# Attention's probabilities times V on narrower TensorE tiles: 12 products a head group instead of 6

## What is computed

```python
SEQ, CHUNK = 256, 64
ATTN_HEADS, ATTN_KV_HEADS, ATTN_HEAD_DIM = 16, 2, 64
# sliding window of 128 keys, in chunks of 64 queries
scores = jnp.einsum('bnqhgd,bnkhd->bnhgqk', qc, kb).astype(jnp.float32) * (ATTN_HEAD_DIM ** -0.5)
...
probs = jax.nn.softmax(jnp.concatenate([scores, sink], axis=-1), axis=-1)[..., :-1]
out = jnp.einsum('bnhgqk,bnkhd->bnqhgd', probs.astype(vb.dtype), vb)
return out.reshape(B, S, ATTN_WIDTH)
```

## Time and profile before

| | |
|---|---|
| median of three runs | 1077.94 us (1077.86 to 1078.0) |
| the profiled execution, own time | 1078.6 us |
| its span, first to last instruction | 1076.9 us |
| TensorE busy | 1072.4 us, 6575 matmuls and 6575 weight loads |
| VectorE, ScalarE, GpSimd busy | 909.0, 635.2, 79.8 us |
| granted TensorE clock, mean | 1.000 of full speed |
| all of `times_v`, as busy time of its two lines | 2.6 us (L2026) and 2.4 us (L2030) |

### The profile page before, as it was taken

The page is one execution under the profiler, slowest core; times in us unless marked ns, Lnnn a source line. Parts: engine busy times, 40 slices in busy tenths (PEclk is TensorE's granted clock), DMA queues, the critical chain, the costliest instruction groups (busy, mean ns, idle before and its releaser), DMA issues.

```text
span 1076.9 us, 18252 instructions
## 1 busy us (share of the span) xinstructions
PE 1072.4 (100%) x6575; PEld 928.2 (86%) x6575; DVE 909.0 (84%) x1376; ACT 635.2 (59%) x930; POOL 79.8 (7%) x114
## 2 busy tenths in 40 slices
PE   9999999999999999999999999999999999999998
PEld 9888888888888888888888888888888888888887
DVE  6878988989655678888888888888877889999997
ACT  7677676756545655555555555545555566656663
POOL 4500000000000000000000000000000000000000
PEclk9999999999999999999999999999999999999999
DMA  8656587877889888798888888789887789798884
GB/s 270 189 165 188 177 231 223 220 226 217 234 268 246 267 246 238 239 252 236 249 230 245 247 247 248 221 255 253 272 236 236 222 280 325 260 303 313 260 296 157
DMA packets 192336, 260.77 MB, mean 242 GB/s; under 512 B 9605, under 2 KB 143894, under 8 KB 192022
## 3 DMA queue, kind: packets, MB, share of 16 engines
q1 hardware_dynamic: 176246, 216.24, 61.9%
q0 software_dynamic: 13344, 38.80, 16.4%
q10 hardware_dynamic: 2688, 5.00, 1.2%
HBM read 255.02 MB, written 43.78 MB: 277 GB/s over the span
## 4 chain that ended last, share of the span: by engine, by line
PE 99%; DMA 1%; DVE 0%; SPq 0%; issue 0%; DVEq 0%
PE bank L1821 38%; PE bank L1829 20%; PE bank L2216 7%; PE bank L2218 7%; PE bank L2217 7%; PE bank L2067 3%; PE bank L1868 3%; PE bank L2068 3%; PE bank L1870 3%; PE bank L1869 3%; PE bank L2069 3%; PE bank L1789 1%; PE bank L1897 1%; DMA xt<-in_x_dram 1%; PE bank L1986 0%; PE bank L2108 0%
## 5 line engine op out<-in xcount | busy, mean ns | idle before, releaser
L792 ACT CAST w_hi<-raw 128x1024 fp32r<-128x1024 f32 x299 | 312.4, 1049 | 252.0 <-PE bank L1829 119.2
L1201 DVE TENSOR_TENSOR w_lo<-raw,w_hi 128x1024 fp32r<-128x1024 f32 x299 | 364.2, 1223 | 107.0 <-ACT w_hi L792 106.4
L1821 PE MATMUL bank<-hs,w_hi 128*128 128x512 f32 x1792 | 423.0, 391 | 0.0
L1821 PEld LDWEIGHTS bank<-hs,w_hi 128*128 128x128 f32 x1792 | 331.6, 188 | 65.9 <-issue 0.7
L1829 PEld LDWEIGHTS bank<-hs,w_lo 128*128 128x128 f32 x1792 | 224.6, 192 | 5.6 <-issue 0.2
L1829 PE MATMUL bank<-hs,w_lo 128*128 128x256 f32 x1792 | 227.3, 283 | 0.0
L1171 ACT CAST hi_slot<-slot 128x1024 fp32r<-128x1024 f32 (+1 forms) x102 | 118.5, 1188 | 62.0 <-PE bank L2218 21.0
L1728 DVE TENSOR_TENSOR slot_lo<-slot,hi_slot 128x1024 fp32r<-128x1024 f32 (+1 forms) x102 | 136.8, 1389 | 6.3 <-ACT hi_slot L1171 4.8
L2218 PE MATMUL bank<-hi_slot,gated 128*128 128x512 f32 (+1 forms) x194 | 75.2, 387 | 0.0
L2216 PE MATMUL bank<-hi_slot,gated 128*128 128x512 f32 (+1 forms) x194 | 75.1, 387 | 0.0
L1646 DVE SCALAR_TENSOR_TENSOR C<-U,cols,C 128x256 f32<-128x256 f32 x176 | 73.4, 480 | 0.0
(11 more groups left out here) (248 smaller groups left out, 1183.2 us busy)
## 6 DMA issues: line engine op xcount, KB each, us to landing
raw<-in_w_ffn_up_dram SPq DMA_DIRECT2D x176, 512.0 KB, 4.8
u_sums<-in_w_ffn_down_dram POOLq DMA_DIRECT2D x58, 512.0 KB, 5.6
raw<-in_w_in_dram SPq DMA_DIRECT2D x51, 512.0 KB, 4.2
slot<-in_w_ffn_down_dram SPq DMA_DIRECT2D x38, 512.0 KB, 4.6
slot<-u_sums SPq DMA_DIRECT2D x74, 256.0 KB, 5.1
raw<-in_w_in_dram SPq DMA_DIRECT2D x66, 256.0 KB, 3.8
raw<-in_w_out_dram SPq DMA_DIRECT2D x32, 512.0 KB, 5.3
u_sums<-u_sums POOLq DMA_DIRECT2D x16, 512.0 KB, 7.4
```

Of the source, the lines that this page charges most:

```text
L792: act.copy(w_hi[:, i, :], raw[:, i, :]).then_inc(units_hi, 1)
L1201: dve.tensor_tensor(w_lo[:, i, :], raw[:, i, :], w_hi[:, i, :].bitcast(F32), ALU.subtract)\
L1821: m = pe.matmul(banks[b][:, :], w_hi[:, i, c], hs[:, 4 * i + k, :], start=(first and k == 0), stop=(final and k == 3))
```

## The change

`times_v` uses tiles of 32 array columns instead of 64. Each half's 64 output partitions are split in two (`r` of 0 and `NARROW`, which is 32), with the matching 32 columns of V as weights, so each product of before becomes two, and each round of two products becomes a round of four. The probabilities that stream past, the output places, the semaphores and the order of the rounds stay as they are. Products per group go from 6 to 12.

```diff
                 kv = g // (Q_GROUPS // KV_HEADS)
-                c = slice(kv * HEAD_DIM, (kv + 1) * HEAD_DIM)
-                o = [banks_o_att[g][half * HEAD_DIM:(half + 1) * HEAD_DIM, :]
-                     .rearrange("p (a t q) -> p a t q", a=2, t=TT) for half in range(2)]
-                for half in range(2):
-                    pe.matmul(o[half][:, :, 0, :], vt[:, 0, c], PT[:, g % 2, 0, half, :, :], start=True, stop=True)
+                o = banks_o_att[g][:, :].rearrange("p (a t q) -> p a t q", a=2, t=TT)
+                parts = [(half, half * HEAD_DIM + r, kv * HEAD_DIM + r) for half in range(2) for r in (0, NARROW)]
+                for half, row, c in parts:
+                    pe.matmul(o[row:row + NARROW, :, 0, :], vt[:, 0, c:c + NARROW], PT[:, g % 2, 0, half, :, :],
+                              start=True, stop=True)
                 for part in range(2):
                     q = slice(part * CHUNK, (part + 1) * CHUNK)
-                    for half in range(2):
-                        last = pe.matmul(o[half][:, :, 1, q], vt[:, 1 + part, c], PT[:, g % 2, 1, half, :, q],
-                                         start=True, stop=True)
+                    for half, row, c in parts:
+                        last = pe.matmul(o[row:row + NARROW, :, 1, q], vt[:, 1 + part, c:c + NARROW],
+                                         PT[:, g % 2, 1, half, :, q], start=True, stop=True)
                 last.then_inc(pv_made, 1)
```

## The result

The changed kernel took 1083.1 us (median of 6 runs, 1080.94 to 1083.68), the kernel before in the same runs 1077.93 (1077.86 to 1078.24): a ratio of 1.0043, 95% interval 1.0032 to 1.0054. It is slower by 0.4%, and its runs scatter over 2.7 us where those of before lie within 0.4. The forecast was 1077.7 with a range of 1077.3 to 1078.4, no difference that can be measured. It was wrong.

What follows compares the result with a forecast made beforehand. TensorE's own time was taken as the bound. Groups 0 and 1 gave -0.25 us, groups 2 and 3 -0.01, together -0.27; from the median of 1077.94 that made 1077.7 us, range 1077.3 to 1078.4.

Steps and rivals of the forecast that it cites:

- What bounds the kernel: Whole span: TensorE bounds it, never waiting for another engine after some 9 us; its time in `times_v` counts one for one.
- The rounds: In `times_v`: four 32-column tiles stream abreast at full rate, rounds cost 0.87 us as before, difference nothing; upper bound +3.5 us.
- Rival 3: In `times_v`: four tiles don't stream abreast at this length, +3.5 us less 0.27, 1081.2 us; chance 0.06.
- Rival 2: In `times_v`: each matmul record has a fixed price, 48 x 9.3 ns = +0.45 us less 0.27, 1078.1 us; chance 0.08.
- The change of form: Ahead of `times_v`: same tile form as `mean_of_queries` removes the pause in groups 0 and 1 (0.10 to 0.01); together -0.27 us.
- rival 1: Ahead of `times_v`: the pause stays, as the engine drains for another reason than tile form; 1077.9 us; chance 0.10.
- the slow first round: First round of `times_v` behind a pause lasts 0.27 against 0.22 us; 0.05 us goes in groups 0 and 1.
- the stagger: Where `times_v` ends, in three places: last tile of the last round starts two records later, +0.013 us each, +0.04 in all.
- Twelve more matmul records and weight loads a group: In `times_v`: their issue and loads hide behind streaming, leaving +0.04 us; without that cover +0.45 us.
- What the gain meets: Behind `times_v`: TensorE may come 0.13 us earlier without meeting a wait; no wait added, no DMA moved.
- the prediction's two signs of being wrong: In the profile after: the rounds stretch, or TensorE waits anywhere behind `times_v` for a unit's splits.
- What I haven't seen: Nowhere in particular: unnamed effects in either direction, given a chance of 0.04 and no size.

Runs made afterwards that it cites:

- the kernel with 160 empty instructions: Changed kernel plus 160 empty TensorE instructions, 20 at each of 8 places, filling 96 to a block of 256: 1077.82 us, ratio 0.9999.
- the run with the moved copies: Changed kernel with the pause of GpSimd's copies in DRAM at units 59 to 67 instead of 30 to 38: 1082.27 us, ratio 1.0041.

## Why the prediction was wrong, step by step

- *What bounds the kernel.* Right for the other engines: from the stop on, every matmul is late by the same 5.08 us to the end, and the 0.2 us gained before it were never lost to another engine. (The two waits of the earlier trace rows are at the start, as it says, but L1789 runs later too, for the transposes at 53 to 97 us.) What it didn't ask is whether TensorE could wait for none of them: for its own instructions.
- *The rounds.* Right: 0.22 and 0.11 us, four abreast. Rival 3 alone named a slowdown that can be told from none, 1081.2 us, but that this lies nearer to the 1083.1 than the forecast is chance, for its mechanism is out: no round stretched, and the kernel with 160 empty instructions has the same rounds in the unchanged time. Rival 2 is out as well: the records cost no time on the array, and the 60 cycles a matmul that it took from the Trainium skill, TensorEngine Tiling (Array Packing), Instruction Overhead, don't show.
- *The change of form.* Right, with one term too small. The pause ahead of `times_v` went in groups 0 and 1 (0.101 to 0.012 us), which puts rival 1 out, and so did the slow first round. Start to start, from the last record before `times_v` to the first behind it: 1.12 to 1.015 us in each of the two, 2.096 to 2.083 us for groups 2 and 3. That is -0.22 us where -0.27 was forecast. Most of the missing 0.05 is the stagger in groups 0 and 1: from the second round on, the four records of a round start over 0.037 us and not 0.020, as the later two follow at 0.013 and 0.018. The kernel with 160 empty instructions is 0.22 us below the kernel before, though its interval takes in no difference.
- *Twelve more matmul records and weight loads a group.* This step failed. It asked what 96 more instructions cost in the queue and on the array, found them hidden, and put the price at nothing, with 0.45 us as the cost without cover. It didn't ask what they do to the supply of all later instructions. The page showed that supply (31 instruction packets of 16 KB on q8), and the trace shows how slow it was: in the kernel before, the block edge in the third stretch passed at 221.97 us, and the next packet started 2.8 us later and landed at 225.68. The list lasted to 231.87, because the edge was at 176 and only 152 of the next 256 instructions were dense. The changed kernel, with its edge at 80, came to the end of its list before the packet had even started. In place of the nothing stand 5.2 us by the medians, with the 0.2 us gained already taken off; the stop took 6.0 us in the trace.
- *What the gain meets.* "No wait is added, and no DMA is moved" was wrong for the same reason: it looked at the splits and the copies, and a wait of 4.2 us was added for an instruction packet. Neither of the prediction's two signs of being wrong showed, as no round stretched and no unit's splits were waited for.
- *The range.* It stood on the terms that were priced, and no rival had a cost away from the changed lines. "What I haven't seen" had 0.04 of the chance; it should have had more, since each added instruction moves every later block edge, and the prediction had not looked at one. That the kernel before has no stop is itself a matter of where its edges happen to fall.

The Trainium skill, Runtime: NRT & Kernel Launch, Instruction fetch mechanics, says that instructions are refilled in blocks of 16 KiB, 256 instructions, and that crossing such a block is mostly hidden because the list is worked off more slowly than it is filled. The blocks agree with the count here. The hiding holds for every crossing in the kernel before, which never stops, but not where an edge falls 48 to 104 instructions into a stretch that takes 328 of them in 2.3 us, 7 ns each: there the crossing cost 0.6 to 5.4 us.

## What to carry to other kernels

An edit that adds or takes away instructions on an engine moves every later block edge of its list; where small instructions stand dense, count the instructions to the edges, and read the instruction packets beside them, before calling an addition free. Here the kernels with an edge between 48 and 104 instructions into the second, third or fourth stretch are 4 to 7 us slower (by medians), and by the table only additions of about 0 to 24 and 231 to 256 instructions keep all four clear, a fifth of all: an estimate from seven shifts, in which the first stretch is taken to behave like the others. When a wait is put down to "issue" far from any edited line, put in empty instructions to fill up the block: it separates what an edit does from where it pushes the rest.

## What the runs showed of the hardware

TensorE goes on 1.2 to 1.5 us after the missing packet has landed, in all nine stops (225.84 to 227.15 us in the changed kernel), so a packet can land before the list runs out and still be late: with 72 instructions added one landed at 225.00 us, TensorE ran dry at 225.74 and went on at 226.34. The granted clock fell with some stops and not with others of nearly the same length: it stayed at 1.00 from 274.5 to 279 us behind the stop of 2.7 us with 48 instructions added, and fell to the lower level (0.50 from 226.0 to 229.3 us) behind the one of 2.4 us in the run with the moved copies. The runs of a kernel that stops scatter over 0.9 to 3.5 us, those of one that doesn't over 0.4 to 1.0. Part of that is the clock: with 48 added the two runs at a mean clock of 1.000 took 1080.59 and 1080.69 us, the four at 0.998 took 1081.95 to 1082.24. That the rest is the fetch's own delay is argued, since each kernel has one trace.
